# Experts of a small encoder trunk: the next weight unit split ahead of the turned products and gathered rows

## The reference, cut to what matters

```python
def swiglu(h, wg, wu, wd):
    return (jax.nn.silu(h @ wg) * (h @ wu)) @ wd

def moe_swiglu(h, w_router, b_router, wg, wu, wd):
    ...
    for e in range(N_EXPERTS):
        out = out + comb[..., e:e + 1] * swiglu(h, wg[e], wu[e], wd[e])
    return out
```

## Time and profile before

| | |
|---|---|
| median of 3 runs | 1880.52 us (1879.57 to 1882.18) |
| profiled execution | 1880.88 us, of which the trace spans 1879.2 us |
| PE busy | 1672.6 us (89%) |
| VectorE busy | 768.6 us (41%) |
| ScalarE busy | 658.9 us (35%) |
| passes 0 to 7 | from 1176.5 to about 1841 us of the span |
| `w_lo`, L1373, VectorE | 146 times, 307.6 us |
| `w_hi`, L1023, ScalarE | 146 times, 256.8 us |
| ScalarE waiting for turned pairs, L1046 | 185.9 us |
| ScalarE waiting for turned rows, L1027 | 100.6 us |

### The profile page before, as it was taken

How to read it: one execution, slowest core, us unless ns; L and a number is a source line. 1 busy time by engine, 2 the same in 40 slices (tenths; PEclk the granted TensorE clock), 3 DMA queues, 4 the chain that set the end, 5 groups by cost and what they waited for, 6 DMA issues and landing times.

```text
span 1879.2 us, 24291 instructions
## 1 busy us (share of the span) xinstructions
PE 1672.6 (89%) x9608; PEld 1384.4 (74%) x9609; DVE 768.6 (41%) x1139; ACT 658.9 (35%) x941; POOL 115.9 (6%) x158
## 2 busy tenths in 40 slices
PE   3888899789999999989599971999999989999995
PEld 1554567689999999966366770888887767789875
DVE  1205341333333323330554231453337777823474
ACT  1305431132222222231363030443327666723361
POOL 1020000000000000000200002001001101010012
PEclk6898999889999999989799965999999999999998
DMA  8245872112212222110940213455338988943384
GB/s 292 117 113 185 330 265 103 67 68 99 96 66 69 70 104 81 64 42 11 318 129 1 90 45 107 168 191 202 119 117 339 348 324 331 351 171 124 134 326 164
DMA packets 87354, 297.82 MB, mean 158 GB/s; under 512 B 12856, under 2 KB 48612, under 8 KB 62756
## 3 DMA queue, kind: packets, MB, share of 16 engines
q1 hardware_dynamic: 79740, 269.56, 41.0%
q0 software_dynamic: 7472, 26.24, 3.8%
HBM read 267.11 MB, written 28.67 MB: 157 GB/s over the span
## 4 chain that ended last, share of the span: by engine, by line
PE 82%; DVE 4%; ACT 4%; DMA 3%; issue 3%; POOL 2%; SPq 1%; ACTq 0%; POOLq 0%; DVEq 0%
PE PS L790 29%; PE PS L704 23%; PE PS L671 7%; PE PS L536 3%; PE PS L509 3%; PE PS L617 2%; PE PS L640 2%; DMA big<-in_ada 2%; PE PS L482 2%; PE PS L741 1%; POOL win L1531 1%; PE PS L629 1%; PE PS L818 1%; PE PS L751 1%; ACT w_hi L1023 1%
## 5 line engine op out<-in xcount | busy, mean ns | idle before, releaser
L1373 DVE TENSOR_TENSOR w_lo<-big,w_hi 128x2048 fp32r<-128x2048 f32 (+1 forms) x146 | 307.6, 2115 | 123.1 <-ACT w_hi L1023 120.5
L1023 ACT CAST w_hi<-big 128x2048 fp32r<-128x2048 f32 (+1 forms) x146 | 256.8, 1768 | 82.8 <-PE PS L790 82.8
L790 PE MATMUL PS<-w_hi,hg_hi 128*128 128x512 f32 (+1 forms) x624 | 240.1, 385 | 13.3 <-DVE w_lo L1373 7.7
L790 PE MATMUL PS<-w_lo,hg_hi 128*128 128x512 f32 (+1 forms) x624 | 234.4, 376 | 0.0
L790 PE MATMUL PS<-w_hi,hg_lo 128*128 128x512 f32 (+1 forms) x624 | 234.3, 376 | 0.0
L704 PE MATMUL PS<-h_hi,dw_hi 128*128 128x288 f32 x704 | 209.3, 297 | 18.9 <-DVE dw_lo L1449 18.9
L704 PE MATMUL PS<-h_hi,dw_lo 128*128 128x288 f32 x704 | 209.2, 297 | 0.0
L704 PE MATMUL PS<-h_lo,dw_hi 128*128 128x288 f32 x704 | 209.0, 297 | 0.0
L994 ACT CAST dw_hi<-big 128x1024 fp32r<-128x1024 f32 (+1 forms) x76 | 70.8, 934 | 284.1 <-PE PS L704 284.1
L1449 DVE TENSOR_TENSOR dw_lo<-big,dw_hi 128x1024 fp32r<-128x1024 f32 (+1 forms) x76 | 82.3, 1085 | 192.3 <-ACT dw_hi L994 192.2
L704 PEld LDWEIGHTS PS<-h_hi,dw_hi 128*128 128x128 f32 x704 | 133.8, 190 | 19.3 <-issue 19.3
(11 more groups left out here) (214 smaller groups left out, 2410.1 us busy)
## 6 DMA issues: line engine op xcount, KB each, us to landing
big<-in_e_w SPq DMA_DIRECT2D x98, 1024.0 KB, 6.0
big<-in_ada SPq DMA_DIRECT2D x48, 1024.0 KB, 6.2
big<-in_e_w SPq DMA_DIRECT2D x48, 768.0 KB, 6.2
big<-in_w_gu SPq DMA_DIRECT2D x22, 1024.0 KB, 4.8
y_slots<-zeros SPq DMA_DIRECT2D x1, 15360.0 KB, 64.0
big<-in_w_dn SPq DMA_DIRECT2D x8, 1408.0 KB, 6.0
big<-in_w_o SPq DMA_DIRECT2D x8, 1024.0 KB, 7.4
y_slots<-big POOLq DMA_DIRECT2D x3, 1536.0 KB, 6.5
```

What stands on the lines that cost most here:

```text
L790: mm = pe.matmul(PS[:, first_bank + t, 0:cols], x_, w_, start=(k == 0 and r == 0), stop=(k == last and r == 2))
L1023: act.copy(w_hi[:, u % 3, 0:w], expert_ring[:, u % MOE_SLOTS, 0:w]).then_inc(hi_done, 1)
L1373: dve.tensor_tensor(w_lo[:, u % 3, 0:w], expert_ring[:, u % MOE_SLOTS, 0:w], w_hi[:, u % 3, 0:w].bitcast(F32), ALU.subtract).then_inc(lo_d ...
```

## The change

In every step of a pass, on ScalarE and on VectorE, the call that splits the weight unit after next moves from behind the turned pair and the gathered rows to a place ahead of them. On ScalarE it now comes first in the step; on VectorE it comes after the product of steps 4, 8 and 12, and ahead of the rest. No instruction is added or removed, no wait is added or removed, and the streams of TensorE, GpSimd and SyncE are the same.

```diff
@@ -1041,12 +1041,12 @@
                 for u in range(UNITS_G):
+                    split_unit(i, u + 2)
                     if u in PAIR_AT:
                         f, m = 2 * PAIR_AT[u], min(2, KF - 2 * PAIR_AT[u])
                         wide(lambda q: act.copy(mt_hi[:, f:f + m, 0:q * P], PS[:, 6:6 + m, 0:q * P]), m_hi, (m_T, i * N_TURNS + PAIR_AT[u] + 1))
                     if u in ROWS_AT:
                         turned_group(i + 1, ROWS_AT[u])
-                    split_unit(i, u + 2)
                     if u < 12 and u % 4 == 2:
```

## The result

The changed kernel takes 1895.7 us in the median (1894.7 to 1898.3) beside 1880.05 us for the kernel before on the same chip. The ratio on record is 1.0089, 95% interval 1.0074 to 1.0104 (the medians alone, 15.7 us apart, give 1.0083). A second measurement gave 1.0094 (1.0080 to 1.0108). The forecast was 1893.5 us in a range of 1886 to 1901: slower, by 13 us where 16 to 17 were measured.

A forecast was written before the change was run, and what follows sets the result against it. TensorE bound three-tile passes; mainly one-tile passes had holes from the splitting engines. Terms 9.0 - 1.75 + 2 x 0.55 + 1.1 + 2.1 + 1.2 + 0.5 = +13.2 us on 1880.5 gave 1893.5, range 1886 to 1901.

The forecast's parts named there:

- Which passes can answer: Only the five one-tile passes, and a little two-tile pass 0, respond to the order; three-tile passes have price zero.
- The hole at step 14: One-tile passes: TensorE waits for turned pair 4's low part, behind unit 15's split; 1.8 us in five passes, +9.0.
- What the other pair steps give back, -1.75: Pair steps other than 14: two old TensorE holes gone, 0.35 us a pass, -1.75 us in all.
- Pass 2: Sign in the changed kernel's trace: this one-tile pass takes 56.8 us and not 54.8.
- The rows of steps 15 and 16: One-tile passes: TensorE waits 1.1 and 1.6 us for low parts of the second and third gathered tiles.
- The end of pass 3: Last pass of the first round: nothing won at the change, step 15's 1.1 us stays, +1.1.
- The end of pass 5: Handover to a three-tile pass, whose first matmul waits for the third tile of rows: 13.9 against 11.7, +2.1.
- The end of pass 7: Last pass; what follows needs the second copy of the result: 1.1 us and a signal, +1.2.
- The clock: TensorE's half-speed spells at 1.7 us each: price between -5 and +5 us, taken as 0.
- The rival that it recovers: Same mechanism and holes, but TensorE's three half-speed spells gone: 1888.5 us, chance 0.22.
- the other ends: Changes of pass after one-tile passes 2 to 5: +0.55 us each at 2 and 4, +1.1 at 3, +2.1 at 5.
- pass 0: Two-tile pass, at its end: +0.7 and +0.3 us of new holes, -0.5 of an old one, +0.5.

The follow-up runs named there:

- VectorE alone: New order in all steps on VectorE, ScalarE keeping the old one, against the kernel before: ratio 1.0528 (1.0512 to 1.0544).
- pairs alone: Split moved first in steps 0 to 14 only, steps 15 to 17 as in the kernel before: ratio 1.0103 (1.0087 to 1.0118).

## Why the prediction was right, and where it was off

- *Which passes can answer*: right. The three-tile passes are 142.3 us as before, the two-tile pass 97.9 against 97.6 (forecast +0.5, measured +0.3, with a hole of 0.47 us on the second tile of rows).
- *The hole at step 14*: right in place and cause, 10.6 us in five (1.9 to 2.5 each), where I had 1.8 each, 9.0: this term was 1.6 us too small. From the end of the pair's low part (1516.23) TensorE took 0.8 us to go on; I had taken the 0.4 to 0.5 of another place.
- *What the other pair steps give back, -1.75*: this term failed. The holes ahead of steps 5, 12 and 13 are 0.31, 0.68 and 0.28 us in pass 3 of the changed kernel and were 0.26, 0.54 and 0.37. Over the five passes all holes in pair steps but the new one come to 5.8 us, before 6.4, so 0.5 us was given back. I had said that those of 5, 12 and 13 come from work that isn't moved, and then took two holes as gone all the same.
- *Step 14's own effect*: not in the prediction, and worth 6 us alone. It didn't spoil the sum only because step 13 hides it, which I hadn't worked out: that is luck.
- *Pass 2*: named as a sign, at 56.8 us, it took 59.5. Its hole at step 14 is 2.45 us and not 1.8, nothing came back in the other pair steps, and a spell of half speed behind that hole cost 1.2.
- *The rows of steps 15 and 16*: 0.85 to 0.87 and 1.37 to 1.45 us, forecast 1.1 and 1.6. From the first rows to the next pass, end of pass 2: 12.45 us (1463.27 to 1475.72), forecast 12.6, before 12.0.
- *The end of pass 3*: TensorE starts pass 4 16.25 us after the first rows (1519.95 to 1536.20), before 13.56, and then waits 1.5 us in unit 2 where it had waited 2.7: together +1.5, forecast +1.1. I had put both of the long waits of the earlier trace rows down to ScalarE's late start of the round; only the one in unit 2 is that. *The end of pass 5*: 13.27 against 11.73, +1.5, forecast +2.1; the hole is on the third tile's low part, as said. *The end of pass 7*: from the first rows to the last matmul 12.42 against 10.18, +2.2, forecast +1.2; the time behind the last matmul got shorter by about 0.4 us.
- *The clock*: taken at nothing, it cost 0.8 and 1.0 us in two traces. A spell was priced at 1.7 us; seven slow matmuls at 0.2 are 1.4. The rival that it recovers fell: the new holes at step 14 had spells in the place of the old ones. The Trainium skill ("TensorE: Matmul & The Clock Gate", section "HAM oscillation — how this bites in real kernels") says that waits between bursts of matmuls throw the clock back, and the traces agree; that shorter waits spare it, as I had concluded from it, they don't bear out: behind the holes of 1.88, 2.37 and 2.45 us at step 14 of passes 4, 5 and 2 the clock fell.

In the profiled executions the passes grew by 18.4 us, 17.6 less the clock. Of the 4.4 us above the sum, 1.2 are what the other pair steps didn't give back, 1.6 the pair's hole and 1.0 the end of pass 7; the other ends and pass 0 came out 0.7 under their terms; 1.2 to 1.3 I can't assign to one place. The mechanism was right, and the sum was low by 2.5 us (medians) to 4.4 (trace); the range held because it reached 7 us to both sides.

## What to carry to other kernels

When two engines split everything that a third one multiplies, the order within a step should go by who is waited for soonest, and not by size or by what is needed next of its kind. Work needed in two units' time (the weights) may not stand ahead of work needed in one (the pair, the rows), if the two together are longer than a unit; here the long subtraction on VectorE decides, and ScalarE's order is free as long as VectorE keeps the old one. Cost each step of a move alone and then together: the holes of neighbouring steps hide each other, and undoing the costliest brings out the next. The same holds for a gain: a pass that starts earlier meets its next wait, here the store of the last result. And who ended a wait is a label, given by time; check it against when that work was really done.

## What the runs showed of the hardware

Behind some of its waits TensorE runs at the lower of its two clock levels (1.2 GHz and not 2.4), in most cases for five to eight full-width matmuls, 1.0 to 1.6 us lost each time; twice it was three and four, and once 13. In 13 traces (all of the table but the one with VectorE alone) there are 40 such spells in the passes, each of them with its first slow matmul within 2.1 us after a hole, the shortest of which is 1.83 us. Of 30 holes over 2.2 us 25 had one, of 31 between 1.6 and 2.2 us 15, of some 95 between 0.8 and 1.6 us none. The same hole of the same program has one in one execution and none in another: 1.83 and 1.86 us at the start of pass 3 in the two traces of the unchanged kernel. So half a microsecond more of waiting can cost two, and a change worth 11.4 us in waits came out at 16.6 in its trace (pairs alone). It is not shown that the spells are why executions of one kernel spread over 3 to 8 us.
